# Order of the long and short products in the later up projections of a two-block fp32 kernel

## The chip, the cores and the metric

One core of a Trainium2 chip runs the whole program. The metric is the device time of one launch in microseconds (us). TensorE is PE in the profile (PEld its weight loads), VectorE is DVE, ScalarE is ACT, GpSimd is POOL, and SyncE is SP, which issues the weight loads from HBM.

## The reference

Two transformer blocks follow each other on 256 tokens of width 2048. The part that matters here is the MLP of the first block, with a hidden width of 8192:

```python
    h = rms_norm(r, g_mlp[i])
    r = r + jnp.square(jax.nn.relu(h @ w_up[i])) @ w_down[i]
    h = rms_norm(r, g_ple[i])
    r = r + jax.nn.sigmoid(h @ w_ple_gate[i]) * (p[i] @ w_ple_proj[i])
```

Everything is float32. Before it the first block has its attention and its short convolution; behind it stands the second block (a convolution module and a SwiGLU). All weight matrices are read once.

## The kernel before

*Precision.* PE multiplies in a faster reduced form of float32 (`F32R`). To keep the accuracy, each operand is split into a high part and a residual: `whi` and `wlo` for weights, and two halves of each row block of A or B for activations. A product x @ w is then x_hi w_hi + x_lo w_hi + x_hi w_lo.

*Units.* Weights come in units of 128x1024 numbers. SyncE loads unit n into one of four slots of `stage` once the residual of unit n-4 is made; ScalarE copies it to `whi` (line 951) once PE has used unit n-4 (`unit_used`); VectorE subtracts and writes `wlo` (line 1513). PE waits for `hi_ready` or `lo_ready` before it uses a unit.

*Panels with weights as stationary operand.* `step` (line 435) computes one panel, 256 output columns, in four units. A unit has four row blocks of 128 (k) for two halves of the panel (m). For each k and m there are two products: a long one (line 458), 512 columns, with `whi` against both halves of the activations, and a short one, 256 columns, with `wlo` against the high half. The long one fills a whole bank of `gp`, the short one adds to its second half. In the plain order the short product follows its long one at once (line 461): alternating pairs. With `hi_first`, or for the one unit `grouped`, the eight long products of a unit come first, and then, behind a wait for `lo_ready`, the eight short ones (line 467). Both orders do the same products. Panels alternate between banks 0 and 1 and banks 2 and 3 (`j`); ScalarE and VectorE take a finished panel out and set `evacuated`, for which the panel after the next one waits. `attn_out` and `conv_out` read B and alternate; `cb`'s second body, `gc` and `w_o` read A and alternate.

*The MLP.* It is done in four rounds. In each, eight up panels read B (the normed activations, ready in all rounds but the beginning of the first), and the hidden values go to `hidden`, which lies in A; then four down panels (`ffn_panel`, line 729; products at lines 743 to 745) read `hidden` as stationary operand, with three products of 512 columns for each pair of blocks, in eight units a panel. Round 0 writes out its first two up panels, the second with an additional wait on `ple_out` (`banks`), and loops over the other six with `up_panels` (line 721), all alternating. Rounds 1 and 2 are one loop over `rnd`, round 3 is written out after it, and in these three all up panels are grouped (`hi_first=True`). Before round 0 PE does the products of `w_ple_proj` (lines 715 to 717, 256 columns) and two sums (`column_sums`, lines 525 and 526, 256 columns each). Behind round 3's down panels comes `gate`, grouped, over B.

*The other engines in an up round.* ScalarE: four conversions, `cross` out of PSUM, the high part of the hidden values. VectorE: four residuals, then add, scale, squared relu, and the hidden residual (up to line 1853). These, and SyncE's loads, have an order of their own, which the change leaves as it is.

*Other names.* `xp` is the second group of four PSUM banks; its bank 1 is not used between the norm before the MLP and the second block. `ones_r` holds ones.

Of the kernel before, what the change touches and what calls it, by code (L numbers as in the profile page):

```python
# [32 lines left out]
P = 128  # L33
D = 2048
T = 256
# [15 lines left out]
HPW = 256  # L51
# [32 lines left out]
def two_block_kernel(nc, io, out):  # L84
    at, _, UNITS = plan()

    with ExitStack() as ctx:
# [9 lines left out]
        B = sb("B", [P, KT, 2 * T], F32R)  # L97
        stage = sb("stage", [P, RING, UNIT])
        whi = sb("whi", [P, RING, UNIT], F32R)
        wlo = sb("wlo", [P, RING, UNIT], F32R)  # L100
# [9 lines left out]
        ones_r = sb("ones_r", [P, P], F32R)  # L110
# [14 lines left out]
        gp = ctx.enter_context(nc.psum_tensor("gp", [P, 4, 512], F32))  # L125
        xp = ctx.enter_context(nc.psum_tensor("xp", [P, 4, 512], F32))
# [51 lines left out]
        spare = A[:].rearrange("p k n -> p (k n)")  # L178
# [77 lines left out]
        r_updated, r_hi, r_ready = sem("r_updated"), sem("r_hi"), sem("r_ready")  # L256
# [175 lines left out]

        @block.tensor
        def _(pe):
            def step(hp, j, n0, M, kt0=0, units=4, slot0=0, ready=None, banks=None, after=None, single=False, hi_first=False, mid=None,
                     grouped=None):

                for u in range(units):
                    slot = (slot0 + u) % RING
                    pe.wait_ge(hi_ready if hi_first else lo_ready, n0 + u + 1)  # L440
                    if u == 0 and not (isinstance(hp, int) and hp == 0):
                        pe.wait_ge(evacuated, XSLOTS + hp - 1)
                        if banks:
                            pe.wait_ge(*banks)
                    for k in range(4):
                        if mid and u in mid and k == 2:
                            mid[u]()
                        if single and u == 0 and k < 2:
                            pe.wait_ge(ready[0], ready[1] + k + 1)
                        elif ready and k % 2 == 0:  # L450
                            pe.wait_ge(ready[0], ready[1] + ready[2] * u + ready[2] // 2 * (k // 2 + 1))
                        kt = kt0 + 4 * u + k
                        first, last = u == 0 and k == 0, u == units - 1 and k == 3
                        for m in range(2):
                            c = k * HPW + m * P
                            hi, lo = whi[:, slot, c:c + P], wlo[:, slot, c:c + P]
                            bank = gp[:, 2 * j + m, :]
                            nc.tensor.matmul(bank.rearrange("p (a t) -> p a t", a=2), hi, both_parts(M, kt),  # L458
                                             start=first, stop=False)
                            if not hi_first and u != grouped:  # L460
                                done = nc.tensor.matmul(bank[:, T:2 * T], lo, M[:, kt, 0:T], start=False, stop=last)  # L461
                    if hi_first or u == grouped:
                        pe.wait_ge(lo_ready, n0 + u + 1)
                        for k in range(4):
                            for m in range(2):
                                c = k * HPW + m * P
                                done = nc.tensor.matmul(gp[:, 2 * j + m, T:2 * T], wlo[:, slot, c:c + P], M[:, kt0 + 4 * u + k, 0:T],  # L467
                                                        start=False, stop=u == units - 1 and k == 3)
                    done.then_inc(unit_used, 1)
                    if after and u in after:  # L470
                        for f in after[u]:
                            f()
# [184 lines left out]
            for t in range(2):  # L657
                done = nc.tensor.matmul(xp[:, 1, t:t + 1], rstd[:, META + t * P:META + t * P + P], ident[:, 0:1],
                                        start=True, stop=True)
# [21 lines left out]
            for phase, kt0, ready in (("attn_out", 0, (attn_ready, HEADS, 0)), ("conv_out", CT, (conv1_ready, 0, 4))):  # L681
                hp0, n0 = at[phase]
# [19 lines left out]
            hp0, n0 = at["ple"]  # L702
            for u in range(4):
                pe.wait_ge(lo_ready, n0 + u + 1)
                for j in range(2):
# [5 lines left out]
                    for m in range(2):  # L711
                        o = gp[:, pair % 4, m * T:m * T + T]
# [5 lines left out]
                    done.then_inc([ple_half, unit_used][j], 1)  # L718
            column_sums(0)
            pe.wait_ge(ple_out, 6)  # L720
            def up_panels(rnd, first_it=0, hi_first=False):

                hp0, n0 = at["up0"]
                with pe.Fori(first_it, 4) as it:
                    for j in range(2):
                        step(hp0 + 12 * rnd + 2 * it + j, j, n0 + 64 * rnd + 8 * it + 4 * j, B, ready=(r_ready, 0, 4),
                             hi_first=hi_first)

            def ffn_panel(rnd, c, j, after=None):

# [33 lines left out]
            def ffn_panels(rnd):  # L764

                with pe.Fori(0, 2) as it:
                    for j in range(2):
                        ffn_panel(rnd, 2 * it + j, j)

            hp0, n0 = at["up0"]  # L770
# [1 line left out]
            step(hp0 + 1, 1, n0 + 4, B, ready=(r_ready, 0, 4), banks=(ple_out, 8))  # L772
            up_panels(0, first_it=1)
            ffn_panels(0)
            with pe.Fori(1, 3) as rnd:
                up_panels(rnd, hi_first=True)
                ffn_panels(rnd)
            up_panels(3, hi_first=True)
            for c in range(4):
                ffn_panel(3, c, c % 2, {1: [turn_ffn(c - 1)]} if c else None)  # L780
            body("gate", 0, B, (r_ready, 16, 4), {0: [turn_ffn(3)], 5: [lambda: column_sums(1)]}, hi_first=True)
# [1744 lines left out]
```

## Time and profile before

| | us |
|---|---|
| median of three runs | 2538.36 |
| lowest and highest | 2536.27, 2539.22 |
| the profiled execution's own time | 2538.74 |
| its span, first to last instruction | 2536.9 |
| PE busy in the span | 2517.5 |
| DVE, ACT, POOL busy | 1711.8, 1237.0, 438.2 |
| read from HBM | 463.20 MB, 183 GB/s |

The four up rounds lie at 670 to 761, 848 to 937, 1024 to 1114 and 1201 to 1290 us of the span, each followed by its down panels; the `gate` stage ends near 1472. Products on PE are pipelined: a product's record has a modelled end and overlaps the next, so a busy share near 100% doesn't say how fast the products follow each other. The distance between two starts does. A group of equal products in the timeline is merged to one row with its count, and an answer on a tile or a line gives the number of products in a window with the first and the last start, from which a mean distance follows.

### The profile page before, as it was taken

How to read it: one execution, taken by the hardware profiler on the slowest of the kernel's cores; microseconds unless marked ns; L12 is line 12 of the kernel's file. 1: busy time of each engine (PE TensorE's matmuls, PEld its weight loads, DVE VectorE, ACT ScalarE, POOL GpSimd, SP SyncE). 2: the span in 40 equal slices, each digit the busy share in tenths (PEclk: the TensorE clock that was granted, in tenths of full speed). 3: DMA queues.
4: the chain of work that ended last, by engine and by line, in shares of the span. 5: the costliest groups of instructions: out<-in, count | busy, mean ns of one | idle time of the engine just before them, and what ended most of it. 6: DMA issues, size and time to landing. Idle time of an engine off the chain costs nothing.

```text
span 2536.9 us, 41160 instructions
## 1 busy us (share of the span) xinstructions
PE 2517.5 (99%) x14121; PEld 2204.2 (87%) x14121; DVE 1711.8 (67%) x2057; ACT 1237.0 (49%) x1522; POOL 438.2 (17%) x297
## 2 busy tenths in 40 slices
PE   9999999999999999999999999999999999999998
PEld 8888888888888888888888899988888888888887
DVE  6568875587765564665667889985766556654665
ACT  6456555554544443443444554455644444444443
POOL 0034410002200000000002378973400000000001
PEclk9999999999999999999999999999999999999999
DMA  7655565665656656566655565536466656565555
GB/s 235 186 168 181 164 187 182 198 193 178 193 181 198 191 188 194 182 197 192 187 180 184 185 175 167 168 111 203 150 196 199 196 179 198 187 190 187 185 180 164
DMA packets 438205, 466.56 MB, mean 184 GB/s; under 512 B 14521, under 2 KB 375475, under 8 KB 437939
## 3 DMA queue, kind: packets, MB, share of 16 engines
q1 hardware_dynamic: 437568, 464.97, 58.9%
q8 instruction: 56, 0.92, 0.1%
q10 hardware_dynamic: 546, 0.38, 0.1%
q14 instruction: 35, 0.29, 0.0%
HBM read 463.20 MB, written 2.10 MB: 183 GB/s over the span
## 4 chain that ended last, share of the span: by engine, by line
PE 88%; DVE 9%; issue 1%; ACT 1%; DMA 0%; POOL 0%; DVEq 0%; ACTq 0%; POOLq 0%; SPq 0%
PE gp L458 39%; PE gp L461 13%; PE gp L467 8%; DVE xp L1975 6%; PE gp L744 5%; PE gp L743 5%; PE gp L745 5%; PE gp L887 3%; PE gp L888 3%; PE gp L886 3%; PE gp L497 1%; DVE wlo L1513 1%; PE gp L646 1%; PE gp L647 1%; PE gp L499 1%
## 5 line engine op out<-in xcount | busy, mean ns | idle before, releaser
L1513 DVE TENSOR_TENSOR wlo<-stage,whi 128x1024 fp32r<-128x1024 f32 x809 | 1016.1, 1271 | 697.2 <-ACT whi L951 693.5
L951 ACT ACTIVATE whi<-stage 128x1024 fp32r<-128x1024 f32 x874 | 914.1, 1057 | 941.4 <-PE gp L461 329.3
L458 PE MATMUL gp<-A,whi 128*128 128x512 f32 x2944 | 959.8, 393 | 0.6 <-DVE wlo L1513 0.3
L458 PEld LDWEIGHTS gp<-A,whi 128*128 128x128 f32 x2944 | 546.8, 188 | 119.0 <-DVE A L1620 0.7
L461 PE MATMUL gp<-A,wlo 128*128 128x256 f32 x2216 | 621.5, 280 | 0.0
L458 PE MATMUL gp<-B,whi 128*128 128x512 f32 x1536 | 435.5, 393 | 0.0
L461 PEld LDWEIGHTS gp<-A,wlo 128*128 128x128 f32 x2216 | 417.5, 188 | 0.0
L458 PEld LDWEIGHTS gp<-B,whi 128*128 128x128 f32 x1536 | 280.4, 188 | 55.5
L743 PE MATMUL gp<-whi,A 128*128 128x512 f32 x512 | 199.5, 390 | 0.0
L744 PE MATMUL gp<-wlo,A 128*128 128x512 f32 x512 | 199.2, 389 | 0.0
L745 PE MATMUL gp<-whi,A 128*128 128x512 f32 x512 | 199.2, 389 | 0.0
L2280 POOL TENSOR_TENSOR sq<-r 128x512 f32 x24 | 29.6, 1232 | 792.0 <-DVE r L1880 685.7
L1975 DVE SCALAR_TENSOR_TENSOR xp<-work,taps,xp 128x256 f32<-128x256 f32 x406 | 164.1, 505 | 1.8 <-PE xp L818 1.8
L2378 POOL TENSOR_TENSOR wlo<-stage,whi 128x1024 fp32r<-128x1024 f32 x64 | 153.9, 2422 | 15.8 <-ACT whi L951 15.4
L800 PE MATMUL gp<-A,whi 128*128 128x272 f32 x512 | 150.9, 295 | 0.5 <-DVE wlo L1513 0.5
L467 PEld LDWEIGHTS gp<-B,wlo 128*128 128x128 f32 x1024 | 139.7, 190 | 10.0
L802 PE MATMUL gp<-A,wlo 128*128 128x272 f32 x512 | 147.7, 288 | 0.0
L801 PE MATMUL gp<-A,whi 128*128 128x272 f32 x512 | 147.4, 288 | 0.0
L461 PE MATMUL gp<-B,wlo 128*128 128x256 f32 x512 | 143.5, 280 | 0.0
L467 PE MATMUL gp<-B,wlo 128*128 128x256 f32 x1024 | 142.8, 282 | 0.0
L888 PE MATMUL gp<-whi,B 128*128 128x512 f32 (+1 forms) x352 | 135.3, 384 | 0.0
L887 PE MATMUL gp<-wlo,B 128*128 128x512 f32 (+1 forms) x352 | 135.3, 384 | 0.0
(344 smaller groups left out, 2864.2 us busy)
## 6 DMA issues: line engine op xcount, KB each, us to landing
stage<-in_w_in SPq DMA_DIRECT2D x160, 512.0 KB, 4.4
stage<-in_w_up SPq DMA_DIRECT2D x128, 512.0 KB, 3.8
stage<-in_w_down SPq DMA_DIRECT2D x128, 512.0 KB, 4.6
stage<-in_ffn_w_gate SPq DMA_DIRECT2D x88, 512.0 KB, 4.6
stage<-in_ffn_w_up SPq DMA_DIRECT2D x88, 512.0 KB, 4.5
stage<-in_ffn_w_down SPq DMA_DIRECT2D x88, 512.0 KB, 4.8
stage<-in_conv_w_in SPq DMA_DIRECT2D x64, 512.0 KB, 4.0
stage<-in_w_o SPq DMA_DIRECT2D x32, 512.0 KB, 4.4
```

Source lines behind the costliest of these rows:

```text
L458: nc.tensor.matmul(bank.rearrange("p (a t) -> p a t", a=2), hi, both_parts(M, kt), start=first, stop=False)
L461: done = nc.tensor.matmul(bank[:, T:2 * T], lo, M[:, kt, 0:T], start=False, stop=last)
L467: done = nc.tensor.matmul(gp[:, 2 * j + m, T:2 * T], wlo[:, slot, c:c + P], M[:, kt0 + 4 * u + k, 0:T], start=False, stop=u == units - 1 a ...
L743: nc.tensor.matmul(o, x_hi, hi, start=kt == 0, stop=False)
L744: nc.tensor.matmul(o, x_hi, lo, start=False, stop=False)
L745: done = nc.tensor.matmul(o, x_lo, hi, start=False, stop=kt == KT - 1)
L887: nc.tensor.matmul(o, x_hi, lo[:, c:c + w], start=False, stop=False)
L888: return nc.tensor.matmul(o, x_lo, hi[:, c:c + w], start=False, stop=last)
L951: nc.scalar.activation(unit_homes(n, slot)[0], stage[:, slot, :], ACT.Copy).then_inc(hi_ready, 1)
L1513: nc.vector.tensor_tensor(lo, stage[:, slot, :], hi.bitcast(F32), ALU.subtract).then_inc(lo_ready, 1)
L1975: nc.vector.scalar_tensor_tensor(dst, x, w, o, ALU.mult, ALU.add).then_inc(tap_done, 1)
L2378: nc.gpsimd.tensor_tensor(wlo[:, slot, :], stage[:, slot, :], whi[:, slot, :].bitcast(F32), ALU.subtract).then_inc(lo_ready, 1)
```

## The change

Rounds 1 to 3 no longer group their products. Each round is written out: its first panel is a `step` with a new argument `head`, its second a plain `step`, the other six come from `up_panels` starting at 1, all alternating. The `head` changes only the first unit of the round's first panel, which `first_unit` issues: in round 1 a spare product of 512 columns (ones against B, into bank 1 of `xp`, read by nobody) goes ahead of it, in round 2 a spare one of 256 columns, and in round 3 the short products lag behind the long ones: h0 h1 l0, h2 l1 h3 l2, h4 l3 h5 l4, h6 l5 h7 l6 l7. `first_unit` has further orders that no round uses. In grouped order a unit's start waited for `hi_ready` and its short products for `lo_ready`; now its start waits for `lo_ready`.

```diff
--- before.py
+++ after.py
@@ -432,8 +432,55 @@
 
         @block.tensor
         def _(pe):
+            def first_unit(head, hp, j, slot, M, kt0, k):
+
+                def high(i, a=0, b=2 * T):
+                    kt, m, c = kt0 + i // 2, i % 2, i // 2 * HPW + i % 2 * P
+                    o = gp[:, 2 * j + m, a:b]
+                    x = M[:, kt, a:b]
+                    return nc.tensor.matmul(o, whi[:, slot, c:c + P], x, start=i < 2, stop=False)
+
+                def low(i):
+                    kt, m, c = kt0 + i // 2, i % 2, i // 2 * HPW + i % 2 * P
+                    return nc.tensor.matmul(gp[:, 2 * j + m, T:2 * T], wlo[:, slot, c:c + P], M[:, kt, 0:T], start=False, stop=False)
+
+                def spare_product(n, width):
+                    for _ in range(n):
+                        nc.tensor.matmul(xp[:, 1, 0:width], ones_r[:], M[:, kt0, 0:width], start=True, stop=True)
+
+                i = 2 * k
+                if head == "thirds" and k or head == "one third" and k == 1:
+                    for n in (i, i + 1):
+                        high(n, 0, T)
+                        high(n, T, 2 * T)
+                        done = low(n)
+                elif head == "two and two":
+                    high(i), high(i + 1), low(i)
+                    done = low(i + 1)
+                elif head == "low first":
+                    if k == 0:
+                        high(0), low(0), high(1)
+                        done = low(1)
+                    else:
+                        low(i), high(i), low(i + 1)
+                        done = high(i + 1)
+                elif head == "lagging":
+                    high(i)
+                    if k:
+                        low(i - 1)
+                    high(i + 1)
+                    done = low(i)
+                    if k == 3:
+                        done = low(7)
+                else:
+                    if k == 0 and head[0] == "spare":
+                        spare_product(head[1], head[2])
+                    high(i), low(i), high(i + 1)
+                    done = low(i + 1)
+                return done
+
             def step(hp, j, n0, M, kt0=0, units=4, slot0=0, ready=None, banks=None, after=None, single=False, hi_first=False, mid=None,
-                     grouped=None):
+                     grouped=None, head=None):
 
                 for u in range(units):
                     slot = (slot0 + u) % RING
@@ -451,6 +498,9 @@
                             pe.wait_ge(ready[0], ready[1] + ready[2] * u + ready[2] // 2 * (k // 2 + 1))
                         kt = kt0 + 4 * u + k
                         first, last = u == 0 and k == 0, u == units - 1 and k == 3
+                        if u == 0 and head:
+                            done = first_unit(head, hp, j, slot, M, kt0, k)
+                            continue
                         for m in range(2):
                             c = k * HPW + m * P
                             hi, lo = whi[:, slot, c:c + P], wlo[:, slot, c:c + P]
@@ -718,13 +768,12 @@
                     done.then_inc([ple_half, unit_used][j], 1)
             column_sums(0)
             pe.wait_ge(ple_out, 6)
-            def up_panels(rnd, first_it=0, hi_first=False):
+            def up_panels(rnd, first_it=0):
 
                 hp0, n0 = at["up0"]
                 with pe.Fori(first_it, 4) as it:
                     for j in range(2):
-                        step(hp0 + 12 * rnd + 2 * it + j, j, n0 + 64 * rnd + 8 * it + 4 * j, B, ready=(r_ready, 0, 4),
-                             hi_first=hi_first)
+                        step(hp0 + 12 * rnd + 2 * it + j, j, n0 + 64 * rnd + 8 * it + 4 * j, B, ready=(r_ready, 0, 4))
 
             def ffn_panel(rnd, c, j, after=None):
 
@@ -772,10 +821,13 @@
             step(hp0 + 1, 1, n0 + 4, B, ready=(r_ready, 0, 4), banks=(ple_out, 8))
             up_panels(0, first_it=1)
             ffn_panels(0)
-            with pe.Fori(1, 3) as rnd:
-                up_panels(rnd, hi_first=True)
-                ffn_panels(rnd)
-            up_panels(3, hi_first=True)
+            for rnd, head in ((1, ("spare", 1, 512)), (2, ("spare", 1, 256)), (3, "lagging")):
+                hp, n = hp0 + 12 * rnd, n0 + 64 * rnd
+                step(hp, 0, n, B, ready=(r_ready, 0, 4), head=head)
+                step(hp + 1, 1, n + 4, B, ready=(r_ready, 0, 4))
+                up_panels(rnd, first_it=1)
+                if rnd < 3:
+                    ffn_panels(rnd)
             for c in range(4):
                 ffn_panel(3, c, c % 2, {1: [turn_ffn(c - 1)]} if c else None)
             body("gate", 0, B, (r_ready, 16, 4), {0: [turn_ffn(3)], 5: [lambda: column_sums(1)]}, hi_first=True)
```

## Rows read from the trace of the kernel before

**Rows 1.** The page: span, PE busy and its granted clock in 40 slices

```profile
span 2536.9 us, 41160 instructions
...
PE 2517.5 (99%) x14121; PEld 2204.2 (87%) x14121; DVE 1711.8 (67%) x2057; ACT 1237.0 (49%) x1522; POOL 438.2 (17%) x297
...
PEclk9999999999999999999999999999999999999999
```

**Rows 2.** The page: the chain that ended last, by engine

```profile
PE 88%; DVE 9%; issue 1%; ACT 1%; DMA 0%; POOL 0%; DVEq 0%; ACTq 0%; POOLq 0%; SPq 0%
```

**Rows 3.** Windows of up rounds 0 to 3: length, then each engine's busy us

```profile
668.00:760.00 92.00, 92.00 (x531) 80.19 (x530) 62.51 (x68) 46.80 (x56) 5.38 (x9) 1.00 0.58 182
847.80:937.00 89.20, 89.20 (x512) 78.46 (x512) 58.48 (x61) 40.55 (x46) 0.00 (x0) 1.00 0.58 184
1024.20:1113.60 89.40, 89.40 (x514) 78.66 (x513) 58.48 (x61) 40.56 (x46) 0.00 (x0) 1.00 0.59 184
1200.60:1290.00 89.40, 89.40 (x514) 78.66 (x513) 58.48 (x61) 40.23 (x46) 0.00 (x0) 1.00 0.59 184
```

**Rows 4.** PE's waits (us, times, longest), and line 458's idle time

```profile
PE xp L549 <- DVE var L1559: 2.6, 2, 1.3
...
PE gp L458 <- DVE wlo L1513: 0.3, 1, 0.3
...
  issue: 0.6, 1
```

**Rows 5.** Short products grouped, round 1: count, ns, first and last start

```profile
L467 PE MATMUL gp<-B,wlo x248: 277/283/283, 849.7 to 934.3; 128*128 128x256 f32 x124
```

**Rows 6.** Short products alternating over B, 480 to 564 us

```profile
L461 PE MATMUL gp<-B,wlo x243: 280/280/280, 479.9 to 563.8; 128*128 128x256 f32 x122
```

**Rows 7.** Short products alternating over A, 372 to 476 us

```profile
L461 PE MATMUL gp<-A,wlo x299: 280/281/281, 371.9 to 475.7; 128*128 128x256 f32 x150
```

**Rows 8.** Short products alternating over B, 684 to 759 us (up round 0)

```profile
L461 PE MATMUL gp<-B,wlo x213: 277/281/284, 684.0 to 758.9; 128*128 128x256 f32 x107
```

**Rows 9.** Timeline of PE in up round 0: start us, duration us

```profile
670.28 0.28 PE L525 MATMUL xp<-A,ones_r 128*128 128x256 f32 x1
670.40 0.28 PE L526 MATMUL xp<-A,ones_r 128*128 128x256 f32 x1
670.52 0.39 PE L458 MATMUL gp<-B,whi 128*128 128x512 f32 x1
670.75 0.28 PE L461 MATMUL gp<-B,wlo 128*128 128x256 f32 x1
...
681.50 0.28 PE L461 MATMUL gp<-B,wlo 128*128 128x256 f32 x1
681.62 0.42 PE L458 MATMUL gp<-B,whi 128*128 128x512 f32 x1
681.88 0.28 PE L461 MATMUL gp<-B,wlo 128*128 128x256 f32 x1
681.99 0.40 PE L458 MATMUL gp<-B,whi 128*128 128x512 f32 x1
682.24 0.28 PE L461 MATMUL gp<-B,wlo 128*128 128x256 f32 x1
682.36 0.40 PE L458 MATMUL gp<-B,whi 128*128 128x512 f32 x1
682.59 0.28 PE L461 MATMUL gp<-B,wlo 128*128 128x256 f32 x1
```

**Rows 10.** Middle product of each down triple, 762 to 846 us

```profile
L744 PE MATMUL gp<-wlo,A x124: 389/389/389, 761.7 to 845.4; 128*128 128x512 f32 x124
```

**Rows 11.** Timeline of PE across the border into up round 1

```profile
847.62 0.39 PE L745 MATMUL gp<-whi,A 128*128 128x512 f32 x1
847.84 1.98 PE L458 MATMUL gp<-B,whi 128*128 128x512 f32 x8
849.66 1.12 PE L467 MATMUL gp<-B,wlo 128*128 128x256 f32 x8
850.61 2.00 PE L458 MATMUL gp<-B,whi 128*128 128x512 f32 x8
852.45 1.11 PE L467 MATMUL gp<-B,wlo 128*128 128x256 f32 x8
```

**Rows 12.** Timeline of VectorE before round 1 and after its first panel

```profile
840.98 1.23 DVE L1513 TENSOR_TENSOR wlo<-stage,whi 128x1024 fp32r<-128x1024 f32 x1 [1.49 <-ACT whi L951]
843.70 1.23 DVE L1513 TENSOR_TENSOR wlo<-stage,whi 128x1024 fp32r<-128x1024 f32 x1 [1.49 <-ACT whi L951]
846.42 1.23 DVE L1513 TENSOR_TENSOR wlo<-stage,whi 128x1024 fp32r<-128x1024 f32 x1 [1.49 <-ACT whi L951]
...
865.31 2.36 DVE L1513 TENSOR_TENSOR wlo<-stage,whi 128x1024 fp32r<-128x1024 f32 x2
```

**Rows 13.** The page: loads of w_up, KB each, us to landing

```profile
stage<-in_w_up SPq DMA_DIRECT2D x128, 512.0 KB, 3.8
```

**Rows 14.** Timeline of PE into down round 0, into up round 2

```profile
760.67 0.28 PE L461 MATMUL gp<-B,wlo 128*128 128x256 f32 x1
760.79 0.40 PE L743 MATMUL gp<-whi,A 128*128 128x512 f32 x1
761.03 0.39 PE L744 MATMUL gp<-wlo,A 128*128 128x512 f32 x1
761.26 0.39 PE L745 MATMUL gp<-whi,A 128*128 128x512 f32 x1
...
1024.04 0.39 PE L745 MATMUL gp<-whi,A 128*128 128x512 f32 x1
1024.27 1.98 PE L458 MATMUL gp<-B,whi 128*128 128x512 f32 x8
```

## The prediction, made before the changed kernel was run

> **What bounds the kernel now.** I read the page first: PE is busy for 2517.5 of 2536.9 us and its clock digits are 9 in all 40 slices [rows 1]; the chain that ended last is 88% PE [rows 2]. So the end moves only if PE's own stream gets shorter or a hole opens in it. Next the windows over the four up projections: in each of them PE is busy from edge to edge (89.20 of 89.20 us), the granted clock is 1.00 of full speed, the 2.4 GHz level, and VectorE (58.48), ScalarE (40.55) and the DMA engines (0.58) have room [rows 3]. The list of PE's waits names twelve holes in the whole run, the longest total 2.6 us, and the only one that a missing residual `wlo` causes in L458's panels is 0.3 us [rows 4]. There is no stall for this change to remove. Busy time can't tell more, because each product's record overlaps the next; what counts is the distance between starts. I took that from the counts of the short products (256 columns) with their first and last start, since each pair, one long and one short product, has one of them, and a unit is eight pairs.
>
> The same sixteen products of a unit are met in four paces:
> - grouped (eight long, then eight short), the order that the change takes away: 248 short products are 31 units; from the first start (849.66, from the timeline) to the last (934.3), less seven steps of 0.12 inside the last group, are 30 units: (84.64 - 0.84)/30 = 2.793 us a unit [rows 5].
> - alternating over B, in `attn_out` and `conv_out`: (563.8 - 479.9)/242 = 0.3467 us a pair, 2.774 a unit [rows 6]. I call this the short rhythm.
> - alternating over A, in `cb` and `gc`: (475.7 - 371.9)/298 = 0.3483, 2.787 a unit [rows 7].
> - alternating over B, in up round 0 after 684 us: (758.9 - 684.0)/212 = 0.3533, 2.826 a unit [rows 8]. I call this the long rhythm.
>
> The last two B cases run the same line over the same tile at the same clock, so the order alone doesn't set the pace: the stream locks into one rhythm or another and keeps it. Round 0 shows the moment. It begins after 256-column products and runs at the short rhythm: from 670.52 to 681.62 are the 32 pairs of its first panel, 11.10 us, 2.775 a unit. The first long product of the second panel (681.62) is then followed by its short partner after 0.26 instead of 0.23 us, and from there on the starts are 0.24, 0.12, 0.23, 0.12 apart, the long rhythm, for the other seven panels [rows 9]. A slip of 0.03 us was enough.
>
> **The change part by part.** It touches PE's stream alone.
>
> *Order of 96 units.* Three rounds of eight panels of four units: 3 x 32 units leave 2.793 us each. In the short rhythm a round gains 32 x (2.793 - 2.774) = 0.61 us; at A's pace 32 x 0.006 = 0.19; in the long rhythm it loses 32 x (2.826 - 2.793) = 1.06. Columns, weight loads and products are the same number; all of this lies on the path, since nothing else ends last. Which rhythm each round takes is the whole question, and no row of before shows alternation over B entered straight from a down panel. What precedes it there is the steadiest stream of the run, long products only, 0.227 apart (83.7/123 = 0.6805 a triple) [rows 10], without a hole at the border [rows 11]. I take the short rhythm, for these reasons: it is the pace of the one stretch that came in without a slip and of the first panel of round 0; long products settle the stream (the first eight of round 1, straight after the down panel, take 1.82 us, the next eight, after short ones, 1.84 [rows 11]); and the thing that slipped in round 0 came with the extra wait on `ple_out`, which only that panel has. The bounds stay: -0.61 and +1.06 a round.
>
> *The spare products.* One of 512 columns in round 1: 0.227 us by the steps of the down panels [rows 10]. One of 256 in round 2: 0.12 us by the steps of the sums just before round 0 [rows 9]. They write a bank that nobody reads in that stretch, read B and `ones_r`, both there since before round 0, and delay everything behind them by their own length, on the path: +0.35 us. They may also be what sets the rhythm; that belongs to the question above.
>
> *The lagging first unit of round 3.* Same eight long and eight short products, each short one later by one place. Two long ones stand together at its start and two short ones at its end: steps of 0.227 and 0.12 that exist anyway. Taken as 0, bounds -0.05 and +0.05.
>
> *Waits that come earlier.* The grouped order let a unit begin with `whi` and asked for `wlo` after 1.82 us (847.84 to 849.66) [rows 11]; now it asks at its start. Who is behind that wait is the whole of PE's queue. Round 1's first unit: ScalarE's and VectorE's conversions run four units ahead, released when a unit is used. The one that starts at 846.42 is for the unit two places after the first of the round, so that of the first unit is two rows earlier, 840.98 + 1.23 = 842.21, 5.6 us before PE needs it [rows 12]. The worst place within a round is after a panel's end, when VectorE does the hidden tail first: two conversions take 865.31 to 867.67, the first of them, done near 866.5, for the unit that PE starts at about 847.84 + 8 x 2.793 = 870.2, 3.7 us early, and the second 5.3 us early [rows 12]. A shorter rhythm moves these by 0.02 a unit. So cost 0; if that cover were gone, each late unit would cost its lateness. Loads of `w_up` land in 3.8 us, issued once the residual four units before is made [rows 13]; they stay where they are. Units are given back at the same place, their end, so ScalarE's and VectorE's work follows as before, and the waits on `evacuated` look two panels back, over 11 us.
>
> *Unrolled rounds.* The loop over rounds 1 and 2 becomes three written-out copies, each with two written-out panels in front of a loop of three. New code is entered without a hole in before: round 0's last pair is followed by the first down panel's products at 0.24 and 0.23 us [rows 14], and at the jump back to round 2's start the steps are 0.23 [rows 14]. Cost 0. The bound from above is PE's one wait for issue in L458, 0.6 us [rows 4], at each of some eight new entries: +4.8. The Trainium skill (Runtime: NRT & Kernel Launch, section Instruction fetch mechanics) says that a taken branch out of the fetched window forces a fetch, which would make the removed outer jump a gain; the row of that jump shows none to be had.
>
> *Sum* in the short rhythm: -3 x 0.61 + 0.35 = -1.5 us. Against the profiled execution's own 2538.74 us (span 2536.9 and 1.8 around it) that is 2537.2. The median of the three runs is 2538.36, 0.4 below the profiled one, so the predicted time is 2536.9 us.
>
> **A rule against it.** Short products stand 0.12 us apart in the groups and never closer than 0.11, while 256 columns at 2.4 GHz are 0.107 [rows 9]. The Trainium skill (TensorE: Matmul & The Clock Gate, sections LDWEIGHTS and What happens when you issue a matmul) gives a weight load columns/1.2 ns, so by an estimate from that page 107 ns for 128 columns, and says that loads are pulled ahead beside a running product. By that rule a load is covered by a short product as well as by a long one, and order has no price: the sum would be the spare products alone. The traces disagree so far, as one order has two paces; but it stays as the third rival.
>
> **The rivals.**
> 1. *The rhythm is missed in one round.* For it: round 0's slip of 0.03 us, and seven of its eight panels in the long rhythm. Against: no wait in the border panels. Time: -2 x 0.61 + 1.06 + 0.35 = +0.2, 2538.5 us. It is the point from which the change turns: gain until no round locks long, loss after.
> 2. *Slower: the long rhythm in two or three rounds.* After a down panel the phase may be wrong in the same way each time, and nothing in a round ever corrected it in before. Price: two rounds +1.9, three rounds 3 x 1.06 + 0.35 = +3.5, so 2540.2 to 2541.9 us. It decides from the second round that locks long.
> 3. *Order is worth nothing or next to it,* at the grouped pace or A's: between +0.35 and 0.35 - 3 x 0.19 = -0.2: 2538.1 to 2538.7 us.
> 4. *New code is fetched late.* +4.8 - 1.5 = +3.3: 2541.7 us. Against: the rows above.
>
> **How the numbers follow.** Short rhythm in all rounds 0.45; one round long 0.20; rival 3 0.17; rival 2 0.13; rival 4 0.03; what I don't see 0.02. The three runs of before lie 2.95 us apart, so a median of a few may stray by about 1.5. The range goes from 2535.0 (the forecast less 1.9, for that scatter and a pace a little better than seen) to 2541.0 (through one and two long rounds, leaving out the three-round case's end). A change of 0.2% is 5.1 us, about what a measurement of this kernel can tell from none. All cases lie within it; I leave 0.02 on each side and 0.96 for no difference.
>
> **What would show it.** In the changed kernel's trace, the counts of short products with first and last start: 0.3467 a pair in each of the three rounds is the forecast, 0.3533 rival 2, 0.348 to 0.349 rival 3. Rounds that now take 32 x 2.774 = 88.8 us from first to last product against 89.4. Before the first product of rounds 1 and 2 one row on `xp`, followed 0.23 and 0.12 us later. No new entry in PE's waits on `wlo`; an entry for issue after a down panel would be rival 4. The stretches behind (down panels, gate, conv2) should keep their paces; if one of them changes its pace, the total is off by a cause that this sum leaves out.

## The result and the profile after

| | us |
|---|---|
| before, median of 18 runs | 2538.27 (2536.27 to 2539.22) |
| changed, median of 18 runs | 2542.05 (2539.99 to 2543.4) |
| ratio | 1.0015, 95% interval 1.0008 to 1.0021 |
| changed, profiled execution and its span | 2541.07, 2539.3 |

The change makes the kernel slower by 3.8 us (0.15%); the forecast was 1.5 us faster, and the range ended at 2541.0. One launch of all those reported here, in the run with round 0's wait moved ahead, took 5081.86 us, twice the others; that run's ratio leaves it out, and its median moves by less than 0.1 us with it.

The page of the changed kernel (span, PE's busy time and its granted clock) looks as it did before, [rows 1]:

```profile
span 2539.3 us, 41121 instructions
...
PE 2520.7 (99%) x14123; PEld 2204.0 (87%) x14123; DVE 1710.9 (67%) x2057; ACT 1237.1 (49%) x1522; POOL 439.5 (17%) x297
...
PEclk9999999999999999999999999999999999999999
```

Clock and busy time can't tell where the time went. Starts of products can. The answers on the short products of the changed kernel, in up rounds 1, 2, 3 and then round 0 (count, min/median/max ns, first and last start us), against [rows 5] and [rows 8]:

```profile
L511 PE MATMUL gp<-B,wlo x240: 277/281/284, 849.4 to 933.8; 128*128 128x256 f32 x120
...
L511 PE MATMUL gp<-B,wlo x241: 277/281/284, 1027.0 to 1111.8; 128*128 128x256 f32 x121
...
L511 PE MATMUL gp<-B,wlo x242: 277/281/284, 1204.5 to 1289.7; 128*128 128x256 f32 x121
...
L511 PE MATMUL gp<-B,wlo x246: 274/277/281, 671.9 to 756.8; 128*128 128x256 f32 x123
```

Rounds 1 to 3 run at (933.8 - 849.4)/239 = 0.3531, 0.3533 and 0.3535 us a pair. That is the long rhythm that round 0 had in the kernel before, 0.3533. Round 0 itself, whose code is the same, is at 84.9/245 = 0.3465 in this execution, the short one. It kept that rhythm although its second panel, which starts at 681.34, was held back just as in [rows 9]: 0.26 us from its first long product to the short one.

```profile
681.34 0.42 PE L508 MATMUL gp<-B,whi 128*128 128x512 f32 x1
681.60 0.27 PE L511 MATMUL gp<-B,wlo 128*128 128x256 f32 x1
681.72 0.40 PE L508 MATMUL gp<-B,whi 128*128 128x512 f32 x1
681.95 0.28 PE L511 MATMUL gp<-B,wlo 128*128 128x256 f32 x1
682.07 0.39 PE L508 MATMUL gp<-B,whi 128*128 128x512 f32 x1
```

The timeline of PE at the entry into round 1, from the last product of the down panel on (start, duration):

```profile
845.87 0.39 PE L794 MATMUL gp<-whi,A 128*128 128x512 f32 x1
846.10 0.39 PE L449 MATMUL xp<-B,ones_r 128*128 128x512 f32 x1
846.33 0.40 PE L441 MATMUL gp<-B,whi 128*128 128x512 f32 x1
846.56 0.28 PE L445 MATMUL gp<-B,wlo 128*128 128x256 f32 x1
846.68 0.39 PE L441 MATMUL gp<-B,whi 128*128 128x512 f32 x1
846.90 0.28 PE L445 MATMUL gp<-B,wlo 128*128 128x256 f32 x1
847.02 0.40 PE L441 MATMUL gp<-B,whi 128*128 128x512 f32 x1
847.25 0.28 PE L445 MATMUL gp<-B,wlo 128*128 128x256 f32 x1
847.37 0.40 PE L441 MATMUL gp<-B,whi 128*128 128x512 f32 x1
847.61 0.28 PE L445 MATMUL gp<-B,wlo 128*128 128x256 f32 x1
847.73 0.40 PE L441 MATMUL gp<-B,whi 128*128 128x512 f32 x1
847.97 0.28 PE L445 MATMUL gp<-B,wlo 128*128 128x256 f32 x1
848.08 0.40 PE L441 MATMUL gp<-B,whi 128*128 128x512 f32 x1
```

The spare product takes 846.10 to 846.33, 0.23 us as priced, with no hole on either side. Then the steps from a long product to its short one are 0.23, 0.22, 0.23, and from 847.37 on 0.24, 0.24, 0.23 in turn. Three pairs into the round the stream is in the three-pair cycle of [rows 9], and it is still in it at the end of the round.

By stage, from the first product of one stage to the first of the next, both timelines give (the spare products are counted with the down stage before them):

| stage | before | changed | difference |
|---|---|---|---|
| up round 0 | 90.28 | 88.79 | -1.49 |
| down 0, with the spare 512 | 87.05 | 87.30 | +0.25 |
| up round 1 | 89.36 | 90.44 | +1.08 |
| down 1, with the spare 256 | 87.07 | 87.17 | +0.10 |
| up round 2 | 89.36 | 90.45 | +1.09 |
| down 2 | 87.07 | 87.10 | +0.03 |
| up round 3 | 89.36 | 90.44 | +1.08 |
| gate | 91.52 | 91.52 | 0 |

The three up rounds and the three down stages with what stands between them sum to 3.25 + 0.38 = +3.6 us, and the medians differ by 3.8. The 0.03 in down 2 is no part of the lagging unit, which lies in up round 3: down stages with no spare product behind them took 87.05 to 87.10 us in all runs. The two profiled executions differ by only 2.3, since round 0 happened to go well in the changed one (-1.49) and what lies ahead of round 0 and behind `gate` adds 0.2.

### The profile page after: what moved, and what is told of

Its sections match the earlier page's. It is cut to its first block, busy times and chain, and to the rows that moved or that the text cites. A ratio compares the mean times of both kernels' runs of the same rounds, so it can differ in the third digit from the quotient of the medians.

```text
span 2539.3 us, 41121 instructions
## 1 busy us (share of the span) xinstructions
PE 2520.7 (99%) x14123; PEld 2204.0 (87%) x14123; DVE 1710.9 (67%) x2057; ACT 1237.1 (49%) x1522; POOL 439.5 (17%) x297
## 4 chain that ended last, share of the span: by engine, by line
PE 88%; DVE 9%; issue 1%; ACT 1%; POOL 0%; DMA 0%; DVEq 0%; ACTq 0%; POOLq 0%
PE gp L508 39%; PE gp L511 16%; DVE xp L2027 6%; PE gp L794 5%; PE gp L792 5%; PE gp L793 5%; PE gp L517 4%; PE gp L939 3%; PE gp L940 3%; PE gp L938 3%; PE gp L547 1%; DVE wlo L1565 1%; PE gp L696 1%; PE gp L697 1%; PE gp L549 1%
## 5 line engine op out<-in xcount | busy, mean ns | idle before, releaser
L508 PE MATMUL gp<-B,whi 128*128 128x512 f32 x1512 | 504.8, 395 | 0.0
L511 PE MATMUL gp<-B,wlo 128*128 128x256 f32 x1256 | 351.6, 280 | 0.0
L511 PEld LDWEIGHTS gp<-B,wlo 128*128 128x128 f32 x1256 | 237.0, 189 | 0.0
L940 PE MATMUL gp<-whi,B 128*128 128x512 f32 (+1 forms) x352 | 135.3, 384 | 0.0
L938 PE MATMUL gp<-whi,B 128*128 128x512 f32 (+1 forms) x352 | 135.2, 384 | 0.0
```

The lines of the kernel that those rows point to most:

```text
L938: nc.tensor.matmul(o, x_hi, hi[:, c:c + w], start=kt == 0, stop=False)
L940: return nc.tensor.matmul(o, x_lo, hi[:, c:c + w], start=False, stop=last)
```

## The experiments

Each is given with what was expected of it; its edit is against the changed kernel unless said otherwise. A round's time is from its first up product to the first down product; 88.75 is the short rhythm throughout, 90.44 the long one, 89.36 the grouped order.

**No head at all.**

```diff
-            for rnd, head in ((1, ("spare", 1, 512)), (2, ("spare", 1, 256)), (3, "lagging")):
+            for rnd, head in ((1, None), (2, None), (3, None)):
```

> The changed kernel with no head at all in rounds 1 to 3: plain alternation from the first unit, straight after the down panels. Theory E (the entry from the long products of a down panel locks alternation over B into the long rhythm, whatever stands at its head): each round's 512 products take 90.4 us, as in the changed kernel, and the total is about 0.4 us below the changed one, the spare products. Theory H (the heads themselves shift the stream into the long rhythm, plain alternation would take the short one): 88.8 us a round, and some 5 us below the changed kernel in total. Theory C (each entry is a matter of chance in every execution): a mixture of 88.8 and 90.4.

Median 2541.48 against 2538.59, ratio 1.0011 (1.0001 to 1.0021). All three rounds 90.44 us. The entry into round 1 (timeline), and then the short products behind it (the answer on the tile):

```profile
846.87 0.39 PE L794 MATMUL gp<-whi,A 128*128 128x512 f32 x1
847.10 0.39 PE L508 MATMUL gp<-B,whi 128*128 128x512 f32 x1
847.33 0.28 PE L511 MATMUL gp<-B,wlo 128*128 128x256 f32 x1
847.44 0.40 PE L508 MATMUL gp<-B,whi 128*128 128x512 f32 x1
847.67 0.28 PE L511 MATMUL gp<-B,wlo 128*128 128x256 f32 x1
847.79 0.40 PE L508 MATMUL gp<-B,whi 128*128 128x512 f32 x1
848.03 0.28 PE L511 MATMUL gp<-B,wlo 128*128 128x256 f32 x1
```

```profile
L511 PE MATMUL gp<-B,wlo x249: 277/281/284, 848.0 to 935.7; 128*128 128x256 f32 x125
```

87.7/248 = 0.3536. The heads did not bring the long rhythm in, and they did not keep it out. Theory H falls. Its median lies 0.6 us under the changed kernel's; the spare products account for 0.35 of that, and medians of this kernel taken at different times differ by more than what is left (the kernel before: 2538.27 to 2538.97).

**Written out but grouped.** All three rounds with `hi_first=True` and without heads.

> Rounds 1 to 3 written out as in the changed kernel, but all units grouped as before, and no heads: the writing-out alone. If the code's form costs nothing (the prediction's step), each round takes 89.36 us as in the kernel before, and the total is that of before within 0.5 us. If the new code is fetched late, a wait for issue of up to 0.6 us stands at the entries and the total is up to 4.8 us above.

Median 2538.82 against 2538.59, ratio 1.0001 (0.9991 to 1.001); rounds 89.36, 89.36, 89.36. Writing the loop out is free, as priced, and the steps at the entries are those of the kernel before (0.23 us). The fourth rival falls with this run.

**Short spare products.**

```diff
+            for rnd, head in ((1, ("spare", 2, 256)), (2, ("spare", 4, 256)), (3, ("spare", 8, 256))):
```

> Heads of two, four and eight spare products of 256 columns in rounds 1, 2 and 3. Theory S (what stands right before the first pair decides: round 0, which comes after 98 products of 256 columns, starts in the short rhythm): from some number of short products on a round takes 88.8 us behind its spare ones, most likely the third, perhaps all. Theory E (see e1_plain): 90.4 us in all three. The spare products themselves should cost 0.12 us each.

90.45, 88.75 and 90.45 us. The down stages with the spares ahead of the rounds grew to 87.29, 87.54 and 88.02, thus by about 0.12 us for each spare product (0.24, 0.47 and 0.95 above 87.05, 87.07 and 87.07). Four of them bring the short rhythm, two and eight don't. So the entry is not bound to be long (theory E falls), and it is not a matter of "enough" short products either.

**Other orders of the first unit.**

```diff
+            for rnd, head in ((1, "low first"), (2, "two and two"), (3, "thirds")):
```

> Three other orders of the first unit: round 1 low first (h0 l0 h1 l1, then l h l h), round 2 two and two (h h l l), round 3 the long products from the second block on in two halves of 256 columns. Theory E: 90.4 us in all three. Theory P (the place in the three-pair cycle at which the stream comes in decides, and some order of the first unit meets the short rhythm): at least one round at 88.8 us.

90.42, 88.75 and 88.84 us: h h l l (two long products, then two short ones) and the order whose long products are halved from the second block on enter the short rhythm, low first does not. Theory P fits so far, but each head had been entered once, and chance was not excluded.

**The same head in all three rounds.**

```diff
+            for rnd, head in ((1, "two and two"), (2, "two and two"), (3, "two and two")):
```

> The changed kernel with the first unit of each of rounds 1 to 3 in the order h h l l, which took the short rhythm once (round 2 of the run with other orders, 88.75 us). Theory P (the head alone decides, the same way in every round and execution): 88.75 us in all three rounds, 3 x 0.61 = 1.8 us below the kernel before and 5.4 us below the changed one. Theory C (chance in each entry) or theory R (round 2 is special; two of the three short rounds so far were round 2): at least one of the rounds at 90.4 us.

88.75, 88.75 and 88.75 us. Median 2536.91 against 2538.69, 1.8 us lower; the ratio's interval, 0.9994 (0.9984 to 1.0003), just takes in 1. So the trace shows the gain in the rounds, and the totals point the same way without showing it by themselves. The entry into round 1, two products to a row, and the pace behind it:

```profile
847.09 0.62 PE L441 MATMUL gp<-B,whi 128*128 128x512 f32 x2
847.54 0.40 PE L445 MATMUL gp<-B,wlo 128*128 128x256 f32 x2
847.77 0.63 PE L441 MATMUL gp<-B,whi 128*128 128x512 f32 x2
848.24 0.39 PE L445 MATMUL gp<-B,wlo 128*128 128x256 f32 x2
848.47 0.62 PE L441 MATMUL gp<-B,whi 128*128 128x512 f32 x2
```

```profile
L511 PE MATMUL gp<-B,wlo x243: 274/280/280, 850.1 to 934.0; 128*128 128x256 f32 x122
...
L511 PE MATMUL gp<-B,wlo x213: 277/281/284, 683.9 to 758.8; 128*128 128x256 f32 x107
```

(934.0 - 850.1)/242 = 0.3467. The last row is round 0 of the same execution, 74.9/212 = 0.3533: both rhythms stand in one trace, over the same tiles and with the same line of code.

**Round 0 with that head too.**

```diff
-            step(hp0, 0, n0, B, ready=(r_ready, 0, 4))
-            step(hp0 + 1, 1, n0 + 4, B, ready=(r_ready, 0, 4), banks=(ple_out, 8))
+            step(hp0, 0, n0, B, ready=(r_ready, 0, 4), head="two and two")
+            step(hp0 + 1, 1, n0 + 4, B, ready=(r_ready, 0, 4), banks=(ple_out, 8), head="two and two")
```

> As the run before, and in round 0 too the first two panels begin with a unit h h l l. Round 0 took 88.8 us once and 90.3 to 90.4 five times with the same code. Theory P: the head sets the rhythm after any entry, so round 0 takes 88.8 us in every execution, the total is a further 1.5 us lower, 3.3 below before. Theory W (the wait on the projection's banks shifts the stream by a time that differs between executions, and the head can't make up for it): 90.4 us again in a part of the executions, and the total is scattered as before.

Rounds 1 to 3, with h h l l as in the run before, at 88.75 again, but round 0 at 90.25: a short first panel (11.12 us) and a long remainder (11.29 to 11.31 each). Median 2536.63 against 2538.69, ratio 0.9994 (0.9985 to 1.0003). The head that works after a down panel did not work at round 0's second panel in this execution.

**Breaks inside a round.** Round 1: h h l l at its head, one spare 256 ahead of the second panel. Round 2: the same with a spare 512. Round 3: plain entry, h h l l in the second panel.

> Heads inside a running round. Rounds 1 and 2 begin with h h l l, and one spare product (256 columns, 512 columns) stands ahead of the second panel; round 3 begins plainly (90.44 us in the plain kernel) and has h h l l in its second panel. Theory L (a rhythm is a stable state, left only by a break in the order): the first panel of round 3 is long, 2.827 a unit, and the other seven short if h h l l cures it, so about 11.3 + 77.6 = 89.0 us; a spare product in rounds 1 and 2 may throw the stream into the long rhythm from the second panel on (90.2 us) or not (88.9 with the spare). Rival: the rhythm is set by what precedes a whole round, and breaks inside it heal: 88.9 in rounds 1 and 2, 90.4 in round 3.

88.88, 88.98 and 90.41 us. A spare product inside the short rhythm costs its own length (0.13 and 0.23) and the rhythm heals. A unit of h h l l, four times over, inside the long rhythm doesn't cure it: the timeline of round 3 (its second panel starts at 1210.71), and the short products from there on:

```profile
1210.36 0.40 PE L508 MATMUL gp<-B,whi 128*128 128x512 f32 x1
1210.59 0.28 PE L511 MATMUL gp<-B,wlo 128*128 128x256 f32 x1
1210.71 0.64 PE L441 MATMUL gp<-B,whi 128*128 128x512 f32 x2
1211.19 0.40 PE L445 MATMUL gp<-B,wlo 128*128 128x256 f32 x2
...
1213.28 0.40 PE L445 MATMUL gp<-B,wlo 128*128 128x256 f32 x2
1213.51 0.40 PE L508 MATMUL gp<-B,whi 128*128 128x512 f32 x1
```

```profile
L511 PE MATMUL gp<-B,wlo x210: 277/281/284, 1214.8 to 1288.7; 128*128 128x256 f32 x105
```

73.9/209 = 0.3536. Each rhythm held against the breaks tried in it, so theory L's forecast, that h h l l cures the long rhythm inside a round, fails. In rounds 1 to 3 the rhythm is set where the round is entered; only round 0 changed it inside, at its second panel.

**Four spare products in rounds 1 and 3, the lagging unit in round 2.**

```diff
+            for rnd, head in ((1, ("spare", 4, 256)), (2, "lagging"), (3, ("spare", 4, 256))):
```

> Four spare products of 256 columns ahead of rounds 1 and 3, which took the short rhythm in round 2 of an earlier run, and the lagging first unit in round 2, which took the long one in round 3. Theory P (the head alone decides): 88.75, 90.45 and 88.75 us. Theory R (round 2 is special): 90.4, 88.8 and 90.4 us. Theory C: any mixture.

88.75, 90.44 and 88.75 us, as theory P says. With the earlier runs, four short spares are short in rounds 1, 2 and 3, lagging is long in rounds 2 and 3: the round's number plays no part. Theory R falls.

**Round 0's extra wait moved ahead of the round**, with h h l l in rounds 1 to 3.

```diff
-            pe.wait_ge(ple_out, 6)
+            pe.wait_ge(ple_out, 8)
...
-            step(hp0 + 1, 1, n0 + 4, B, ready=(r_ready, 0, 4), banks=(ple_out, 8))
+            step(hp0 + 1, 1, n0 + 4, B, ready=(r_ready, 0, 4))
```

> The kernel with h h l l at the head of rounds 1 to 3, and round 0's wait for the projection's last banks taken from its second panel to before its first (8 instead of 6 evacuated before PE goes on). Theory W (the third wait at the head of round 0's second panel holds its first product back by some 0.03 us and so throws the stream into the long rhythm): round 0 begins as before in one of the rhythms and keeps it for all eight panels, 88.75 us where it begins short; some two microseconds may be lost in waiting before the round, for ScalarE's last two copies. Rival theory V (the second panel of round 0 slips for another reason, such as new code): it goes long at its second panel without that wait too, 90.3 us.

Round 0 takes 88.86 us, rounds 1 to 3 88.75 each. Median 2536.40 against 2538.72, ratio 0.999 (0.9981 to 0.9999): the one version whose interval lies below 1, and 2.3 us under the kernel before. The timeline at round 0's start, with the new wait in brackets, and the place of the second panel (its first product is the one at 681.66):

```profile
669.73 0.28 PE L576 MATMUL xp<-A,ones_r 128*128 128x256 f32 x1
670.46 0.50 PE L508 MATMUL gp<-B,whi 128*128 128x512 f32 x1 [0.45 <-ACT work L1226]
670.80 0.28 PE L511 MATMUL gp<-B,wlo 128*128 128x256 f32 x1
...
681.55 0.28 PE L511 MATMUL gp<-B,wlo 128*128 128x256 f32 x1
681.66 0.39 PE L508 MATMUL gp<-B,whi 128*128 128x512 f32 x1
681.89 0.27 PE L511 MATMUL gp<-B,wlo 128*128 128x256 f32 x1
682.01 0.40 PE L508 MATMUL gp<-B,whi 128*128 128x512 f32 x1
682.24 0.28 PE L511 MATMUL gp<-B,wlo 128*128 128x256 f32 x1
```

```profile
L511 PE MATMUL gp<-B,wlo x246: 274/277/280, 671.8 to 756.8; 128*128 128x256 f32 x123
```

PE now waits 0.45 us for ScalarE's last copy, and the 0.26 step of [rows 9] is gone from the second panel (0.23 now); 85.0/245 = 0.3469 is kept. The first step of the round is 0.34 us (670.46 to 670.80), a longer delay than the one at the second panel ever was, and the short rhythm sets in behind it all the same.

**The same kind of wait elsewhere.** The kernel with h h l l in rounds 1 to 3, plus one wait on `ple_out` that is long satisfied: in round 1 at the second panel's start (`banks`, just as in round 0), in round 2 ahead of the first product, in round 3 ahead of the loop.

> h h l l at the head of rounds 1 to 3, and one more wait that is long satisfied: in round 1 at the start of the second panel, as round 0 has it; in round 2 ahead of the first product; in round 3 between the second panel and the loop of the others. Theory W (one more wait holds a product back and throws the stream out of the short rhythm): rounds 1 and 3 turn long at that place, 90.3 and about 90.2 us, round 2 perhaps. Rival V: a satisfied wait costs nothing, 88.75 us in all three.

88.75, 88.75 and 88.75 us. A satisfied wait costs nothing there and throws nothing, and no longer step stands at the second panel of round 1 either (858.68 to 858.91, 0.23 us). Theory W in its general form falls.

**More heads.** A grouped first unit in round 1, three spare products of 256 in round 2, two of 512 in round 3.

> Three more heads, straight after a down panel: round 1 a grouped first unit (eight long, eight short), round 2 three spare products of 256 columns (one, two and eight took the long rhythm, four the short one), round 3 two spare ones of 512 (one took the long one). By the picture that what stands before matters only through the place at which the stream comes in, long spares are like the down panel's own and change nothing: 90.4 us in round 3. For the grouped unit and the three short ones the picture gives no forecast; the grouped one costs 0.02 more in its own unit, so 88.8 or 90.4 us.

90.40, 90.46 and 88.76 us. The forecast for two long spares was wrong: none and one are long, two are short. I had no picture that says why.

**The wait moved, in the kernel before.** Grouped rounds 1 to 3; only the edit of `ple_out`.

> The kernel before, grouped rounds and all, with only the wait for the projection's last banks moved from round 0's second panel to ahead of its first. In the run with both edits round 0 took 88.86 us and PE waited 0.5 us more ahead of it, but a satisfied wait did no harm in rounds 1 to 3, so it is open whether that wait is what makes round 0 slip. If it is: round 0 at 88.9 us here too, the stage before it 0.6 longer, and the total some 0.8 us below before with less scatter. If that one profile was luck: round 0 at 90.3 or 90.4 us and the total 0.6 above before.

Round 0 88.86 us again, rounds 1 to 3 89.36, the stage ahead 102.16 instead of 101.55. Median 2537.57 against 2538.97, ratio 0.9996 (0.9987 to 1.0006). The short products of its round 0:

```profile
L461 PE MATMUL gp<-B,wlo x246: 274/277/280, 672.8 to 757.8; 128*128 128x256 f32 x123
```

85.0/245 = 0.3469. The interval takes in 1. The profiled execution itself took 2538.87 us, as it reached `attn_out` 0.67 us later than the kernel before did (479.27 against 478.60); round 0 isn't all of the scatter.

With the wait at the second panel there are twelve profiled executions (these kernels, before and changed). Three were long in round 0 from the first unit. The other nine began short, and in all nine the second panel was held back: 0.25 to 0.27 us from its first long product to the short one, or 0.24 between its first two long ones where it began with h h l l. Eight went over to the long rhythm there and one, the changed kernel's, did not, with a step of 0.26 that the others had too. With the wait ahead of the round there is no such step, and two of two are short. So the wait there goes with the slip, nine to none, and the slip mostly but not always with the long rhythm. Two executions are few, and both also had the pause of 0.45 us ahead of the round.

What a head did, all entries after a down panel in the profiled executions, each listed with the number of entries. A head that was entered more than once always gave the same rhythm; for those entered once nothing more is shown than that one entry:

| head | rhythm |
|---|---|
| none | long, 4 of 4 |
| spare 512: one / two | long, 1 / short, 1 |
| spare 256: one / two / three / four / eight | long, 1 / long, 1 / long, 1 / short, 3 of 3 / long, 1 |
| lagging | long, 2 of 2 |
| low first | long, 1 |
| grouped first unit | long, 1 |
| halved long products | short, 1 |
| h h l l | short, 15 of 15 |

## Why the prediction was wrong

*Right:* that PE's stream alone sets the end; the four paces and their prices (+1.06 a round was forecast for the long rhythm, +1.08 came; -0.61 for the short one, and 88.75 against 89.36 came in the kernels that took it); the spare products (0.23 and 0.12 between starts in the timeline, against 0.227 and 0.12); the lagging unit (its round took 90.44 us, as the rounds without a head did, so 0); the earlier waits for `wlo` (PE's list of waits has no new entry on it); the writing-out at nothing, shown by the grouped kernel. The median of the kernel with h h l l, 1.8 us under before, is what the sum gives for three short rounds without spares, and the changed kernel's 2542.05 is close to the second rival's three-round time, 2541.9.

The third rival, that order has no price, falls with rounds of 88.75, 89.36 and 90.44 us for the same products. The Trainium skill (TensorE: Matmul & The Clock Gate, section LDWEIGHTS) gives a weight load columns/1.2 ns, by an estimate from that page 107 ns for 128 columns, from which the prediction drew that every order would run alike; these runs disagree with what was drawn from it. The records of the loads themselves last 188 to 189 ns in the mean, in the short rhythm and in the long one, and don't tell the two apart. The Trainium skill's rule on taken branches (Runtime: NRT & Kernel Launch, section Instruction fetch mechanics) shows nothing here either way, since grouped rounds take 89.36 us with the outer loop's jump and without it.

*Wrong:* one step, the choice in "Order of 96 units" between its two bounds. I took the short rhythm for the entry from a down panel, at -0.61 us a round, and without a head this entry is long, four times out of four (three in the plain kernel, one in the run with breaks inside a round); behind the three heads of the change it is long too, at +1.08 us a round. None of the three reasons holds. The stretches in which alternation over B was short had come out of alternation over A or out of 256-column products, not out of long ones, so they were no neighbours of the unknown entry. The long products do run evenly up to the border, 0.227 apart, but from there the plain pairs are in the long cycle by the third pair. And the slip in round 0 was read as the fault of one wait. The wait does go with the slip, but the sentence "A slip of 0.03 us was enough" doesn't hold: the changed kernel's own round 0 had the same slip and stayed short, and rounds 1 to 3 were long without any slip or wait. That a rhythm was lost so easily should have raised the chance of all three rounds being long together. The three rounds were not three chances of their own either: all enter from the same stream, and a head that was tried more than once acted the same way each time. I would now give "all long" about as much as "all short", not a part of 0.13, and the range, which was cut below that case by choice, had to reach past 2541.9.

*Open:* why a head ends in one rhythm or the other. Order, count and length of what precedes all matter (one and two 512-column spares differ, so do three, four and eight of 256), nothing of it is monotonic, and the records of products and loads don't show what the engine was held by. The cause of the two rhythms is therefore not shown, only what they cost and which entries lead to them. Open too is why the wait at round 0's second panel goes with a slip, and the same wait in round 1 does not; in round 0 the stream had been entered in another way, and the runs with the wait ahead also put a pause before the round, so no run separated these. Another layout of B, as A's, over which the stretch of [rows 7] ran at 0.3483, was not tried.

## What to carry to other kernels

When busy time and waits say nothing, divide the distance of first and last start by the count of products: two orders of the same products, or the same order entered in two ways, can differ by up to 2% in pace on an engine that is never idle. Such a pace can be a state that a whole loop keeps, as here, so measure the entry you mean to use, in every loop, before you price it; an average of neighbouring stretches, or the belief that a settled stream enters well, is no price. Here a changed order in one of a round's 32 units, which costs nothing by itself, decided about 1.7 us a round (90.44 or 88.75 us). Where such a head is found to work, use the same one everywhere rather than an untried one in each loop; the whole gain over the grouped order was 1.8 us of 2538, so it is worth the trouble only where nothing larger is left.

## What the hardware showed that was not expected

- The same instructions over the same tiles, at a granted clock of 1.00, run in either of two lasting rhythms: 88.75/32 = 2.773 us a unit of sixteen products (short) or 90.44/32 = 2.826 (long, a cycle of three pairs). In rounds 1 to 3 both outlive panel borders, loop jumps, and waits that are satisfied; the short one heals after a spare product (88.88 and 88.98 us a round), the long one outlives a unit of h h l l (90.41).
- Behind a down panel the entry decides and is repeatable: h h l l gave the short rhythm at 15 entries of 15, no head the long one at four of four.
- A step of 0.26 us at the second panel of round 0 was followed by the long rhythm in the kernel before and by the short one in the changed kernel, with the same code.
- Round 0 differs between executions of the same code, 88.79 to 90.44 us. The kernel with both edits, whose four rounds all were short in the profile, took 2536.40 us, 2.3 under the kernel before; the changed kernel was 3.8 above it, with the same products but for the two spare ones.
